# Memory queries and half of the gates through the opening's quarter products; first convolution tap on ScalarE, product with the sigmoid on GpSimd

## The chip, the core and the metric

The kernel runs on one core of a Trainium2 chip, on five engines that each work through their own queue of instructions in order and wait for each other through semaphores: PE (TensorE, matmuls), DVE (VectorE), ACT (ScalarE), POOL (GpSimd) and SP (SyncE, which here issues the DMAs). The metric is the device time of one launch in microseconds.

## The reference

One layer of a decoder, in float32, over 1024 tokens of width 1024. What the change touches is the combined input projection and what is taken from it:

```python
u = rms_norm(h, norm_mix_pre[layer])
proj = u @ w_in[layer]
sb_qkv, z, xbc_raw, dt_raw, mem_q, gate_logits = jnp.split(proj, SPLIT_POINTS, axis=-1)
...
y_sb = stick_breaking_attention(to_heads(q), to_heads(k), to_heads(v))
# ssd_branch:
xbc = jax.nn.silu(causal_depthwise_conv(xbc_raw, conv_w, conv_b))   # 4 taps per channel
y = y.reshape(b, s, SSD_INNER) * jax.nn.silu(z)
y_mem = mem_cross_attention(mem_q, mem, norm_mem[layer], w_mem_kv[layer])
```

Stick-breaking attention weighs a key by `sigmoid(z)` times the product of `1 - sigmoid(z)` over the keys between it and the query; per head and per block of 128 queries that is a running product (a scan) along the keys. After the three branches come their merge, an output projection and an MLP.

## The kernel before, in words

`proj` has 96 blocks of 128 columns: q 0 to 7, k 8 to 15, v 16 to 23, z (the gates of the SSD branch) 24 to 39, x, B and C (the convolved ones) 40 to 63, the memory's queries 64 to 71, the merge's gate logits 72 to 95. Each float32 matmul is made as three passes on rounded halves (hi x hi, hi x lo, lo x hi), so a block of 128 columns over all 1024 tokens costs 8 x 3 x 2 = 48 matmuls of 128x512.

**The opening stage** (`front`, until about 336 us) normalizes x, transposes it, makes blocks 0 and 1, the decays and the memory's keys and values (16 items of 24 matmuls each), and then makes pairs of blocks with Strassen-like quarter products: the pair's 2x2 quarters come out of seven products p1 to p7 of 12 matmuls, 84 in place of 96. There are 11 pairs (blocks 2 to 23). POOL makes sums of weight quarters (`weight_sums`), ACT rounds them (`round_front`, `round_back`), DVE takes the rests (`rest_of_front`, `rest_of_back`) and adds the products up (`c11`, `make_u2`, ...).

**The stick-breaking stage** (`stick_breaking`, from about 336 to 1089 us) runs over 16 heads x 8 blocks of queries = 128 steps. Step i with t = i mod 8 (called t=0 to t=7 below) handles (t+1)*128 keys: PE makes the scores (L1301, `sb_psz`), ACT two sigmoids of them (L1395 into `sb_rest`, L1399 into `sb_beta`), DVE the scan over `sb_rest` (L1509), POOL the product of both (L1451). Two steps later PE transposes the weights (`turn`, L1260, `sb_pst`), ACT rounds them (L1362), DVE takes the rest (L1459, `sb_wtl`), each in units of up to four blocks over two PSUM buffers: a transpose waits until the rest of the unit two before is taken. Every four steps PE multiplies the weights with the values (`weigh_values`, L1317, `sb_psy`), and ACT and DVE (L1493) move that out.

Between these, PE makes the blocks 24 to 71 as direct products (`project`, L1279, `sb_psg`): 48 blocks, 48 matmuls each. The list AT_STEP says how many of them each step of a head gets: 11 at t=0 up to 25 at t=7, 144 a head. They stand in PE's program in two halves, one ahead of the step's transposes and one behind. Each kind of block has a tail that is put at steps counted from the one in which the block ends (`ends`): a convolved block ("x") is copied by ACT, then on DVE the first tap (L1469) and the second (L1473) one step later, the other two taps two steps later, a sigmoid on ACT three later (L1386), the product with it on DVE four later (L1479), the store five later. A gate block ("z") has its sigmoid on ACT and its product on DVE (L1484) at once; a query block ("q") is copied and stored. The order in every engine's program is fixed by these loops; within a step DVE has the scan, then the rests of the transposed weights, then the tails.

With 144 matmuls a head, three blocks end in each head: in t=3, t=5 and t=7. Kinds run "xzxzxq", so a convolved block ends at t=5 in one head and at t=3 and t=7 in the next. The weights' blocks come through a two-slot ring: SP loads, POOL rounds (L1429) and takes the rest (L1437).

The later stages (SSD, merge, output projection, MLP) read `scratch_proj` and are not touched.

## Time and profile before

| | us |
|---|---|
| median of 3 runs | 2694.46 (2691.84 to 2698.86) |
| the profiled execution | 2688.13 |
| its span | 2686.4 |
| opening stage up to the first step's block products | 0 to 336.5 |
| stick-breaking stage | 336.5 to 1088.9 |

The clock granted to PE over the profiled execution was 0.99 of full speed. In the page a group's row is: line, engine, operation, output<-inputs, shapes, count | busy us, mean ns of one | idle time of the engine before it and what ended it. A timeline row is: start us, length us, engine, line, operation, names, count, and in brackets the idle time before and what ended it. A row of the windows is: from:to in us, length; then for PE, PEld (weight loads), DVE, ACT and POOL the busy us and the number of instructions; then the clock granted to PE (1.00 is 2.4 GHz, 0.50 is 1.2 GHz), the share of time that DMA was busy, and GB/s. A matmul's length includes its way through the array; the time that it takes of PE is the distance from its start to the next one's.

### The profile page before, as it was taken

How to read it: one execution, taken by the hardware profiler on the slowest of the kernel's cores; microseconds unless marked ns; L12 is line 12 of the kernel's file. 1: busy time of each engine (PE TensorE's matmuls, PEld its weight loads, DVE VectorE, ACT ScalarE, POOL GpSimd, SP SyncE). 2: the span in 40 equal slices, each digit the busy share in tenths (PEclk: the TensorE clock that was granted, in tenths of full speed). 3: DMA queues.
4: the chain of work that ended last, by engine and by line, in shares of the span. 5: the costliest groups of instructions: out<-in, count | busy, mean ns of one | idle time of the engine just before them, and what ended most of it. 6: DMA issues, size and time to landing. Idle time of an engine off the chain costs nothing. (4 is left out here: it accounts for less than half of the span.)

```text
span 2686.4 us, 35512 instructions
## 1 busy us (share of the span) xinstructions
PE 2597.0 (97%) x12752; PEld 2175.4 (81%) x12752; DVE 1850.0 (69%) x2063; ACT 1191.2 (44%) x2098; POOL 1313.1 (49%) x809
## 2 busy tenths in 40 slices
PE   7999999999999999799999899999998999999998
PEld 6888888888888888688888777878887788888886
DVE  5666476777677677498888656653258887768567
ACT  5533144444444444467666544443144222244443
POOL 3233255454554554288888743545600676535224
PEclk9999999999999999899999999999999999999999
DMA  4634443433324341467666653434331444376574
GB/s 160 204 151 160 153 149 105 126 102 109 112 94 134 110 119 62 137 175 210 196 207 202 226 189 133 152 134 149 126 126 55 150 160 166 129 245 211 203 253 146
DMA packets 208108, 411.53 MB, mean 153 GB/s; under 512 B 19648, under 2 KB 100160, under 8 KB 207936
## 3 DMA queue, kind: packets, MB, share of 16 engines
q1 hardware_dynamic: 207936, 409.27, 46.0%
q8 instruction: 104, 1.70, 0.3%
q14 instruction: 68, 0.56, 0.1%
HBM read 289.01 MB, written 120.19 MB: 152 GB/s over the span
## 5 line engine op out<-in xcount | busy, mean ns | idle before, releaser
L1451 POOL TENSOR_TENSOR sb_beta<-sb_beta,sb_rest 128x128 f32<-128x128 f32 (+7 forms) x128 | 164.1, 1282 | 371.4 <-DVE sb_rest L1509 371.4
L1279 PE MATMUL sb_psg<-uh,sb_wl 128*128 128x512 f32 x768 | 309.7, 403 | 0.0
L1279 PE MATMUL sb_psg<-ul,sb_wh 128*128 128x512 f32 x768 | 304.3, 396 | 0.0
L1279 PE MATMUL sb_psg<-uh,sb_wh 128*128 128x512 f32 x768 | 302.8, 394 | 0.0
L3169 PE MATMUL ff_ps<-ff_mh,ff_total 128*128 128x512 f32 x896 | 278.6, 391 | 4.6 <-DVE ff_total L3672 4.6
L1509 DVE TENSOR_TENSOR_SCAN sb_rest<-sb_rest 128x128 f32<-128x128 f32 (+7 forms) x128 | 187.3, 1463 | 115.1 <-ACT sb_rest L1395 114.8
L3169 PEld LDWEIGHTS ff_ps<-ff_mh,ff_total 128*128 128x128 f32 x896 | 169.4, 189 | 41.0 <-issue 5.7
L2314 PE MATMUL first_ps<-uh,mg_wh 128*128 128x512 f32 x480 | 193.3, 403 | 6.2 <-DVE ul L2519 4.9
L2314 PE MATMUL first_ps<-ul,mg_wh 128*128 128x512 f32 x480 | 188.5, 393 | 0.0
L2314 PE MATMUL first_ps<-uh,mg_wl 128*128 128x512 f32 x480 | 188.3, 392 | 0.0
L3169 PE MATMUL ff_ps<-ff_ml,ff_total 128*128 128x512 f32 x448 | 175.2, 391 | 0.0
L1362 ACT ACTIVATE sb_wth<-sb_pst 128x512 fp32r<-128x512 f32 (+1 forms) x192 | 87.3, 490 | 189.9 <-PE sb_pst L1260 186.6
L1279 PEld LDWEIGHTS sb_psg<-ul,sb_wh 128*128 128x128 f32 x768 | 144.4, 188 | 29.9
L1279 PEld LDWEIGHTS sb_psg<-uh,sb_wl 128*128 128x128 f32 x768 | 144.6, 188 | 25.4
L1279 PEld LDWEIGHTS sb_psg<-uh,sb_wh 128*128 128x128 f32 x768 | 144.9, 189 | 24.0
L1801 PE MATMUL first_ps<-uh,ssd_gwh 128*128 128x512 f32 x384 | 155.0, 404 | 5.9 <-ACT ssd_out L1866 5.0
L1801 PE MATMUL first_ps<-ul,ssd_gwh 128*128 128x512 f32 x384 | 151.5, 395 | 0.0
L1801 PE MATMUL first_ps<-uh,ssd_gwl 128*128 128x512 f32 x384 | 151.2, 394 | 0.0
L1459 DVE TENSOR_TENSOR sb_wtl<-sb_pst,sb_wth 128x512 fp32r<-128x512 f32 (+1 forms) x192 | 99.6, 546 | 74.3 <-ACT sb_wth L1362 74.3
L2292 POOL TENSOR_TENSOR merged<-merged,mg_gate 128x1024 f32<-128x1024 f32 x24 | 61.3, 2553 | 159.6 <-DVE mg_gate L2526 159.6
L1473 DVE SCALAR_TENSOR_TENSOR sb_out<-sb_padded,sb_cw,sb_out 128x1024 f32<-128x1024 f32 x72 | 131.7, 1829 | 1.7
L1395 ACT ACTIVATE sb_rest<-sb_psz 128x128 f32<-128x128 f32 (+7 forms) x128 | 83.6, 653 | 108.6 <-PE sb_psz L1301 107.7
(422 smaller groups left out, 7259.6 us busy)
## 6 DMA issues: line engine op xcount, KB each, us to landing
sb_w<-in_w_in SPq DMA_DIRECT2D x48, 512.0 KB, 4.4
scratch_proj<-sb_out SPq DMA_DIRECT2D x48, 512.0 KB, 2.9
ff_w<-in_w_down SPq DMA_DIRECT2D x96, 256.0 KB, 3.4
sb_k<-scratch_qk SPq DMA_DIRECT2D x64, 256.0 KB, 6.1
ssd_arow<-scratch_decay SPq DMA_DIRECT2D x32, 512.0 KB, 5.6
mg_gate<-scratch_proj SPq DMA_DIRECT2D x32, 512.0 KB, 3.6
ff_w<-in_w_up SPq DMA_DIRECT2D x32, 512.0 KB, 3.7
mg_w<-in_w_branch SPq DMA_DIRECT2D x30, 512.0 KB, 4.5
```

Of the source, the lines that this page charges most:

```text
L1279: last = nc.tensor.matmul(ps_g[:, h], l[:, s, k], r[:, k, h * HALF:(h + 1) * HALF], start=(k == 0 and j == 0), stop=(k == KB - 1 and j == 2))
L1362: nc.scalar.activation(out, src, ACT.Copy).then_inc(hi_done, 1)
L1395: nc.scalar.activation(rest[:, i % 3, 1:cols + 1], ps_z[:, 0:cols], ACT.Sigmoid, scale=-0.125).then_inc(keep_done, 1)
L1451: nc.gpsimd.tensor_tensor(beta[:, i % 3, 0:cols], beta[:, i % 3, 0:cols], rest[:, i % 3, 0:cols], ALU.mult).then_inc(weighted, 1)
L1459: nc.vector.tensor_tensor(out, src, hi, ALU.subtract).then_inc(lo_done, 1)
L1473: nc.vector.scalar_tensor_tensor(out_tile[:, 0], padded[:, tap:tap + S], cw[:, n, tap:tap + 1], out_tile[:, 0], ALU.mult, ALU.add).then_in ...
L1509: nc.vector.tensor_tensor_scan(kept, kept, kept, 1.0, ALU.mult, ALU.bypass).then_inc(scanned, 1)
L1801: last = nc.tensor.matmul(ps_g[:, h], l[:, s, k], r[:, k, h * HALF:(h + 1) * HALF], start=(k == 0 and j == 0), stop=(k == KB - 1 and j == 2))
L2292: nc.gpsimd.tensor_tensor(merged[:, n % KB], merged[:, n % KB], gate[:, n % 2], ALU.add).then_inc(summed, 1)
L2314: last = nc.tensor.matmul(ps[:, s, cols], l[:, k], r[:, k, cols], start=(k == 0 and j == 0), stop=(k == KB - 1 and j == 2))
L3169: done = nc.tensor.matmul(down_bank(p, local), l[:, columns(local)], r, start=(begins and c == 0 and j == 0), stop=(c == PAIRS - 1 and j = ...
```

## The change: what it does, and the diff

1. Eight pairs move from the stick stage to the opening: blocks 24 to 31 (half of the z gates) and 64 to 71 (the memory's queries). The opening has 19 pairs in place of 11. For the four gate pairs ACT takes the sigmoid and DVE multiplies, before the tile is stored.
2. The stick stage keeps 32 blocks, kinds "xxxz", 96 matmuls a head (AT_STEP 5 to 19). Two blocks end in each head: the first in t=5, the second in t=7. The first is always a convolved block; the second is one in every other head and a gate block in the rest.
3. The first tap goes from DVE to ACT (`first_tap`, an activation with scale and bias) in the step in which the block ends; DVE keeps one tap in the next step and two in the one after. The product with the sigmoid goes from DVE to POOL (`silu`), ahead of POOL's other work of its step. `padded` is doubled, and `out_tile` is used by the number of the block.
4. In the opening DVE's and ACT's order changes: the rest of a normalized tile is taken right behind its scaling, the decays are taken out one tile earlier in the loop, the third memory item's rest comes ahead of the first blocks' low halves, the rounding of the four sums of u (`round_t`) is spread over items 2, 5, 8, 11, and the first pair's factors are made at items 13 and 14.

```diff
+Z_EARLY = 8
...
-    BLOCK_PAIRS = [(b, b + 1) for b in range(2, Z0, 2)]
+    BLOCK_PAIRS = [(b, b + 1) for b in (*range(2, Z0 + Z_EARLY, 2), *range(MQ0, G0, 2))]
...
+    FIRST_GATED, N_GATED = (Z0 - 2) // 2, Z_EARLY // 2
...
+    T_ITEMS = (2, 5, 8, 11)
...
+        def sigm_of_tile(c, row):
+            act.wait_ge(c22_made if row else c11_made, c + 1)
+            act.wait_ge(c21_made if row else c12_made, c + 1)
+            act.wait_ge(hi_stored[row], 16 * N_SPLIT)
+            if c > FIRST_GATED:
+                act.wait_ge(gated, gates_to(c - 1, row))
+            nc.scalar.activation(sigm[:, row], tiles[:, 2 * (c % 2) + row], ACT.Sigmoid).then_inc(tile_sigm, 1)
...
+        round_kv(2)
         hi_of_first(0)
-        round_kv(2)
         hi_of_first(1)
         for m in range(N_KV):
-            if 1 <= m <= 4:
-                round_t(m)
+            if m in T_ITEMS:
...
-            if m == 15:
+            if m == 13:
                 round_front(0)
+            if m == 14:
+                for which in (S1, S2, S3):
+                    round_back(which, 0)
                 act.wait_ge(sumsT_out, 1)
                 nc.scalar.activation(grownT, sumsT, ACT.Exp).then_inc(grown_out, 1)
-        for which in (S1, S2, S3, A22, S4):
+        for which in (A22, S4):
             round_back(which, 0)
...
+            if c and is_gate(c - 1):
+                for row in range(2):
+                    sigm_of_tile(c - 1, row)
...
+        def gate_of_tile(c, row):
+            dve.wait_ge(tile_sigm, gates_to(c, row))
+            x = tiles[:, 2 * (c % 2) + row]
+            nc.vector.tensor_tensor(x, x, sigm[:, row], ALU.mult).then_inc(gated, 1)
...
-        for i in range(TILES + 2):
-            if i >= 3:
-                rest_of_u(i - 2)
-            if i < TILES:
-                invert(i)
-            if 0 < i <= TILES:
-                scale_turned(i - 1)
-            if i == 2:
+        for i in range(2):
+            invert(i)
+        scale_turned(0)
+        for i in range(1, TILES):
+            if i == 1:
                 rest_of_u(0)
-            if i == TB - 2:
+                scale_turned(1)
+                rest_of_u(1)
+                invert(2)
+            else:
+                scale_turned(i)
+                if i + 1 < TILES:
+                    invert(i + 1)
+                rest_of_u(i)
+            if i == TB - 3:
                 take_decays(0)
         rest_of_kv(0)
         rest_of_kv(1)
+        rest_of_kv(2)
         lo_of_first(0)
-        rest_of_kv(2)
         lo_of_first(1)
         take_decays(1)
         for m in range(N_KV):
-            if 1 <= m <= 4:
-                rest_of_t(m)
             if m + 3 < N_KV:
                 rest_of_kv(m + 3)
+            if m in T_ITEMS:
+                rest_of_t(T_ITEMS.index(m) + 1)
...
-            if m == 15:
+            if m == 13:
                 rest_of_front(0)
+            if m == 14:
+                for which in (S1, S2, S3):
+                    rest_of_back(which, 0)
                 dve.wait_ge(sums_turned, 1)
                 dve.wait_ge(first_stored, 64)
                 nc.vector.tensor_copy(sumsT, ps_csT).then_inc(sumsT_out, 1)
-        for which in (S1, S2, S3, A22, S4):
+        for which in (A22, S4):
             rest_of_back(which, 0)
...
-    rest, padded = sb("rest", [P, 3, S + 1]), sb("padded", [P, CONV - 1 + S])
+    rest, padded = sb("rest", [P, 3, S + 1]), sb("padded", [P, 2, CONV - 1 + S])
...
-    kinds = "xzxzxq"
+    kinds = "xxxz"
...
-    AT_STEP = (11, 13, 15, 17, 19, 21, 23, 25)
+    AT_STEP = (5, 7, 9, 11, 13, 15, 17, 19)
...
-        return {"x": p * 3 + X0 + x // 2, "z": p * 2 + Z0 + x // 2, "q": p + MQ0}[kinds[x]]
+        return X0 + convs_before(m) if kind_of(m) == "x" else Z0 + Z_EARLY + gates_before(m)
...
-                if i == ends(m, 1) + {"x": 5, "z": 2, "q": 1}[kind_of(m)]:
+                if i == ends(m, 1) + {"x": 5, "z": 2}[kind_of(m)]:
...
+        def first_tap(m):
+            n, s = convs_before(m), m % 2
+            act.wait_ge(drained[0], n + 1)
+            act.wait_ge(drained[1], n + 1)
+            if n == 0:
+                act.wait_ge(small_loaded, 32)
+            if m >= 2:
+                act.wait_ge(g_stored[s], (m // 2) * 16)
+            nc.scalar.activation(out_tile[:, s], padded[:, n % 2, 0:S], ACT.Identity, scale=cw[:, n, 0:1],
+                                 bias=cb[:, n:n + 1]).then_inc(tapped, 1)
...
-            act.wait_ge(conv_step, (m // 2 + 1) * CONV)
-            if m >= 2:
-                act.wait_ge(silu_done, m // 2)
-            nc.scalar.activation(sigm[:], out_tile[:, 0], ACT.Sigmoid).then_inc(sigm_done, 1)
+            n = convs_before(m)
+            act.wait_ge(conv_step, (n + 1) * TAPS)
+            if n:
+                act.wait_ge(silu_done, n)
+            nc.scalar.activation(sigm[:], out_tile[:, m % 2], ACT.Sigmoid).then_inc(sigm_done, 1)
...
+                if kind_of(m) == "x" and ends(m, 1) == i:
+                    first_tap(m)
...
+        def silu(m):
+            pool.wait_ge(sigm_done, convs_before(m) + 1)
+            nc.gpsimd.tensor_tensor(out_tile[:, m % 2], out_tile[:, m % 2], sigm[:], ALU.mult).then_inc(silu_done, 1)
...
+            for m in range(FILL):
+                if kind_of(m) == "x" and i == min(ends(m, 1) + 4, N - 1):
+                    silu(m)
...
-                if tap == 0:
-                    for h in range(2):
-                        dve.wait_ge(drained[h], m + 1 - gates_before(m))
-                    if n:
-                        dve.wait_ge(g_stored[0], n * 16)
-                    nc.vector.tensor_scalar(out_tile[:, 0], padded[:, 0:S], cw[:, n, 0:1], cb[:, n:n + 1],
-                                            ALU.mult, ALU.add).then_inc(conv_step, 1)
+                if tap == 1:
+                    dve.wait_ge(tapped, n + 1)
                 else:
-                    dve.wait_ge(conv_step, n * CONV + tap)
-                    nc.vector.scalar_tensor_tensor(
-                        out_tile[:, 0], padded[:, tap:tap + S], cw[:, n, tap:tap + 1],
-                        out_tile[:, 0], ALU.mult, ALU.add).then_inc(conv_step, 1)
-
-        def silu(m):
-            dve.wait_ge(sigm_done, m // 2 + 1)
-            nc.vector.tensor_tensor(out_tile[:, 0], out_tile[:, 0], sigm[:], ALU.mult).then_inc(silu_done, 1)
...
-                    convolve(m, range(2))
+                    convolve(m, range(1, 2))
                 if kind_of(m) == "x" and i == end + 2:
                     convolve(m, range(2, CONV))
-                if kind_of(m) == "x" and i == end + 4:
-                    silu(m)
                 for h in range(2):
                     if kind_of(m) == "z" and i == ends(m, h):
```

How the orders read, in three places.

DVE, stick stage, from the scan of t=7 to the rest of the weights of t=7 (`sb_wtl<-sb_pst 128x4x128 x2`, which the product with the values waits for); before, a head whose convolved block ended at t=5 (the operation named SCALAR_TENSOR_TENSOR on `sb_rest` is the scan):

```order
L1509 SCALAR_TENSOR_TENSOR sb_rest<-sb_rest 128x1024
L1459 TENSOR_TENSOR sb_wtl<-sb_pst,sb_wth 128x4x128
L1459 TENSOR_TENSOR sb_wtl<-sb_pst,sb_wth 128x2x128
L1473 SCALAR_TENSOR_TENSOR sb_out<-sb_padded,sb_cw,sb_out 128x1024 x2
L1509 SCALAR_TENSOR_TENSOR sb_rest<-sb_rest 128x128
L1459 TENSOR_TENSOR sb_wtl<-sb_pst,sb_wth 128x4x128
L1459 TENSOR_TENSOR sb_wtl<-sb_pst,sb_wth 128x3x128
L1509 SCALAR_TENSOR_TENSOR sb_rest<-sb_rest 128x256
L1459 TENSOR_TENSOR sb_wtl<-sb_pst,sb_wth 128x4x128 x2
```

The same place in the changed kernel, a head with two convolved blocks:

```order
L1565 SCALAR_TENSOR_TENSOR sb_rest<-sb_rest 128x1024
L1524 TENSOR_TENSOR sb_wtl<-sb_pst,sb_wth 128x4x128
L1524 TENSOR_TENSOR sb_wtl<-sb_pst,sb_wth 128x2x128
L1533 SCALAR_TENSOR_TENSOR sb_out<-sb_padded,sb_cw,sb_out 128x1024 x2
L1565 SCALAR_TENSOR_TENSOR sb_rest<-sb_rest 128x128
L1524 TENSOR_TENSOR sb_wtl<-sb_pst,sb_wth 128x4x128
L1524 TENSOR_TENSOR sb_wtl<-sb_pst,sb_wth 128x3x128
L1533 SCALAR_TENSOR_TENSOR sb_out<-sb_padded,sb_cw,sb_out 128x1024
L1565 SCALAR_TENSOR_TENSOR sb_rest<-sb_rest 128x256
L1524 TENSOR_TENSOR sb_wtl<-sb_pst,sb_wth 128x4x128 x2
```

DVE's list there is the same plus one tap. In the heads whose second block is a gate, a gate's product (`sb_out<-sb_psg,sb_out 128x512`) stands in front of the scan of t=0 instead of that tap.

PE, from the transposes of the weights of t=7 (at t=1) to the product with the values (L1317) at t=2, before:

```order
L1260 MATMUL sb_pst<-ident,sb_beta 128x128 x8
L1279 MATMUL sb_psg<-uh,sb_wl 128x512
L1279 MATMUL sb_psg<-uh,sb_wh 128x512
L1279 MATMUL sb_psg<-ul,sb_wh 128x512
L1279 MATMUL sb_psg<-uh,sb_wl 128x512
L1279 MATMUL sb_psg<-uh,sb_wh 128x512
L1279 MATMUL sb_psg<-ul,sb_wh 128x512
L1279 MATMUL sb_psg<-uh,sb_wl 128x512
L1301 MATMUL sb_psz<-sb_k,sb_q 128x384
L1300 MATMUL sb_psz<-sb_hiddenr,sb_identr 128x128
L1301 MATMUL sb_psz<-sb_k,sb_q 128x384
L1317 MATMUL sb_psy<-sb_wth,sb_v 128x512
```

The same place in the changed kernel:

```order
L1306 MATMUL sb_pst<-ident,sb_beta 128x128 x8
L1325 MATMUL sb_psg<-uh,sb_wl 128x512
L1325 MATMUL sb_psg<-uh,sb_wh 128x512
L1325 MATMUL sb_psg<-ul,sb_wh 128x512
L1325 MATMUL sb_psg<-uh,sb_wl 128x512
L1347 MATMUL sb_psz<-sb_k,sb_q 128x384
L1346 MATMUL sb_psz<-sb_hiddenr,sb_identr 128x128
L1347 MATMUL sb_psz<-sb_k,sb_q 128x384
L1363 MATMUL sb_psy<-sb_wth,sb_v 128x512
```

Four block products stand between the two where seven stood. From the scores of t=7 to the product with the values at t=2 there are 31 (19 + 5 + 7) where there were 49 (25 + 11 + 13); up to the transposes of the weights of t=7 there are 27 where there were 42.

DVE in the opening, around the decays (COPY), before:

```order
L870 TENSOR_TENSOR fr_f_hi<-fr_ps,fr_gains 128x1024
L887 COPY fr_p<-fr_ps 32x512
L876 TENSOR_TENSOR ul<-fr_f_hi,uh 128x8x128
L854 RECIPROCAL fr_stats<-fr_stats 128x1
L858 TENSOR_SCALAR fr_f_sums<-fr_f_back,fr_stats 128x1024
```

and in the changed kernel:

```order
L882 RECIPROCAL fr_stats<-fr_stats 128x1
L886 TENSOR_SCALAR fr_f_sums<-fr_f_back,fr_stats 128x1024
L904 TENSOR_TENSOR ul<-fr_f_hi,uh 128x8x128
L915 COPY fr_p<-fr_ps 32x512
L898 TENSOR_TENSOR fr_f_hi<-fr_ps,fr_gains 128x1024
```

The rest of the tile (`ul`), for which PE's next products wait, no longer stands behind the copy of the decays, which itself waits for 24 matmuls of PE.

## Rows read from the trace of the kernel before

**Rows 1.** Page, part 1: busy us (share of span) and instructions.
```profile
PE 2597.0 (97%) x12752; PEld 2175.4 (81%) x12752; DVE 1850.0 (69%) x2063; ACT 1191.2 (44%) x2098; POOL 1313.1 (49%) x809
```
**Rows 2.** Windows: opening's slow spell, its steady pairs, the whole stick stage.
```profile
46.60:48.00 1.40, 1.40 (x7) 1.40 (x8) 1.36 (x3) 0.00 (x0) 0.00 (x0) 0.54 0.00 0
48.00:50.00 2.00, 2.00 (x11) 2.00 (x11) 0.88 (x2) 1.44 (x2) 1.40 (x2) 0.50 0.00 0
150.00:200.00 50.00, 50.00 (x222) 41.44 (x221) 33.23 (x41) 17.23 (x24) 12.44 (x9) 1.00 0.50 190
336.50:1088.90 752.40, 750.12 (x3812) 631.22 (x3811) 537.82 (x518) 337.55 (x610) 377.87 (x222) 1.00 0.35 109
```
**Rows 3.** Waits of PE, 336 to 1090: waited for, us, times, longest.
```profile
PE sb_psz L1301 <- ACT sb_beta L1399: 1.9, 1, 1.9
PE sb_psy L1317 <- DVE sb_wtl L1459: 0.4, 1, 0.4
```
**Rows 4.** Timeline of PE, one passage: start, length, instruction [idle before].
```profile
609.46 0.39 PE L1301 MATMUL sb_psz<-sb_k,sb_q 128*128 128x512 f32 x1
...
610.49 0.39 PE L1279 MATMUL sb_psg<-uh,sb_wl 128*128 128x512 f32 x1
...
613.22 0.82 PE L1260 MATMUL sb_pst<-ident,sb_beta 128*128 128x128 f32 x6
...
622.24 1.04 PE L1260 MATMUL sb_pst<-ident,sb_beta 128*128 128x128 f32 x8
...
625.18 0.40 PE L1317 MATMUL sb_psy<-sb_wth,sb_v 128*128 128x512 f32 x1
```
**Rows 5.** Timeline of DVE, the same passage.
```profile
612.33 2.29 DVE L1509 TENSOR_TENSOR_SCAN sb_rest<-sb_rest 128x1024 f32<-128x1024 f32 x1
614.54 1.00 DVE L1459 TENSOR_TENSOR sb_wtl<-sb_pst,sb_wth 128x512 fp32r<-128x512 f32 x2
615.45 3.65 DVE L1473 SCALAR_TENSOR_TENSOR sb_out<-sb_padded,sb_cw,sb_out 128x1024 f32<-128x1024 f32 x2
619.02 0.42 DVE L1509 TENSOR_TENSOR_SCAN sb_rest<-sb_rest 128x128 f32<-128x128 f32 x1
619.64 1.16 DVE L1459 TENSOR_TENSOR sb_wtl<-sb_pst,sb_wth 128x512 fp32r<-128x512 f32 x2 [0.20 <-ACT sb_wth L1362]
621.49 0.89 DVE L1509 TENSOR_TENSOR_SCAN sb_rest<-sb_rest 128x256 f32<-128x256 f32 x1 [0.69 <-ACT sb_rest L1395]
623.51 1.29 DVE L1459 TENSOR_TENSOR sb_wtl<-sb_pst,sb_wth 128x512 fp32r<-128x512 f32 x2 [1.14 <-ACT sb_wth L1362]
```
**Rows 6.** Timelines of ACT and POOL, the same passage.
```profile
610.69 1.03 ACT L1395 ACTIVATE sb_rest<-sb_psz 128x1024 f32<-128x1024 f32 x1 [2.53 <-PE sb_psz L1301]
...
619.87 1.06 ACT L1386 ACTIVATE sb_sigm<-sb_out 128x1024 f32<-128x1024 f32 x1
...
614.70 2.00 POOL L1451 TENSOR_TENSOR sb_beta<-sb_beta,sb_rest 128x1024 f32<-128x1024 f32 x1 [5.00 <-DVE sb_rest L1509]
```
**Rows 7.** Timelines of DVE and POOL, the same place one head later.
```profile
669.45 1.28 DVE L1473 SCALAR_TENSOR_TENSOR sb_out<-sb_padded,sb_cw,sb_out 128x1024 f32<-128x1024 f32 x1
...
672.43 4.49 DVE L1473 SCALAR_TENSOR_TENSOR sb_out<-sb_padded,sb_cw,sb_out 128x1024 f32<-128x1024 f32 x2
...
672.11 2.41 POOL L1437 TENSOR_TENSOR sb_wl<-sb_w,sb_wh 128x1024 fp32r<-128x1024 f32 x1
```
**Rows 8.** Groups by line, DVE in the stick stage.
```profile
L1469 DVE TENSOR_SCALAR sb_out<-sb_padded,sb_cw,sb_cb 128x1024 f32<-128x1024 f32 x24 | 41.0, 1706 | 3.2 <-DMA scratch_proj<-sb_out 3.2
L1479 DVE TENSOR_TENSOR sb_out<-sb_out,sb_sigm 128x1024 f32<-128x1024 f32 x24 | 46.3, 1927 | 0.0
L1484 DVE TENSOR_TENSOR sb_out<-sb_psg,sb_out 128x512 f32<-128x512 f32 x32 | 21.8, 680 | 0.0
```
**Rows 9.** Timeline of PE in the opening: two gaps.
```profile
46.59 0.48 PE L562 MATMUL fr_ps<-uh,fr_fh 128*128 128x256 f32 x1 [1.90 <-DVE ul L876]
...
126.24 0.47 PE L583 MATMUL fr_ps<-uh,fr_fh 128*128 128x512 f32 x1 [2.77 <-DVE fr_fl L905]
```

53 lines of the change are left out of this document (33 added, 20 removed).

## The prediction

> **What bounds the kernel now.** I read the page's busy shares first: PE is busy for 97% of the span, the next engine, DVE, for 69% [rows 1]. So the question is what PE does, and whether others begin to hold it up. Then windows by stage: the steady part of the opening has PE busy 50.00 of 50 us with 222 matmuls, and in the stick stage PE is busy 750.12 of 752.4 us [rows 2]. The waits say the same: PE waits 1.9 and 0.4 us there in all [rows 3]. Both stages are bound by PE's matmuls, so taking matmuls away shortens them, until another chain comes due first. Which one that is the averages hide (DVE is busy 537.82 of 752.4 us in the stick stage, 71% [rows 2]), so I read the timelines of one passage where DVE's work is densest: from the scores of t=7 at 609.46 to PE's product with the values at 625.18 [rows 4 to 6].
>
> In it PE comes to the product at 625.18 - 609.46 = 15.72 us. What it needs then, the rest of the weights of t=7 on DVE, ends at 623.51 + 1.29 = 624.80, that is at 15.34 [rows 5]. The slack is 0.38 us. Of the 15.34 us DVE idles only 0.20 + 0.69 + 1.14 = 2.03 us, waiting for ACT, which waits for PE; and its scan of t=7 starts at 612.33 though ACT had delivered at 610.69 + 1.03 = 611.72 [rows 5, 6]. So DVE's own chain could be done at 15.34 - 2.03 = 13.31, and 0.61 us earlier still if it were free for the scan at once: 12.70.
>
> **The change part by part.** *Matmuls taken from the stick stage.* 16 blocks x 48 = 768. Twelve of them stand between 610.49 and 613.22 [rows 4]: 0.2275 us each, 174.7 us.
>
> *Matmuls added to the opening.* 8 pairs x 84 = 672, at 50 / 222 = 0.2252 us [rows 2]: 151.3 us. Net -23.4 us. This holds if the pairs stay bound by PE: in the steady window DVE is busy 33.2 and ACT 17.2 of 50 us, 2.6 pairs long. A gate pair asks two sigmoids (1.06 each [rows 6]) and two products (1.93 on DVE [rows 8]), in the places where the q and k pairs have two roundings and two subtractions; a query pair asks none of it. Cost zero; if that cover failed, 4 x 3.9 = 15 us. The two weight loads per pair go on at the same pace behind SP.
>
> *Opening's order.* The PE gap of 1.90 us before 46.59 is DVE's copy of the decays standing ahead of the rest of the tile; it goes. Behind it PE ran at a granted clock of 0.50 (1.2 GHz), from 46.6 to 50 us [rows 2, 9], which costs half of 3.4, about 1.7 us; it goes too. The gap of 2.77 us before 126.24 [rows 9] goes because the first pair's factor is made at item 13. Against it, the third tile is now scaled for transposing only behind a rest on DVE, ahead of PE's first products: its eight transposes (1.04 us when warm [rows 4]), about +1.4 at the start's slower pace. Together -5 (bounds -9 to +2; what is late next is the transposes' own chain). ACT's table for the sigmoid is loaded in the opening in place of the 1.9 us wait of rows 3: -1.
>
> *Tails in the stick stage.* DVE loses 24 first taps (41.0 us), 24 products (46.3) and 16 of 32 half gate products (10.9) [rows 8]; 537.8 - 98.2 = 440 us remain, for a stage of 752.4 - 174.7 = 578 us: 76%, where it was 71%. ACT gains 24 x 1.06 = 25 us and stays below 65%. POOL loses 16 blocks' rounding and rests, gains 24 products at about 2.0 (its product of the same shape took 2.00 [rows 6]) and stays near 63%. No engine becomes the bound on average.
>
> *The dense passage.* The blocks end at t=5 and t=7, so the two late taps still stand at t=7, DVE's list from there to the rest of the weights of t=7 is as before, and none of the 98 us was in it. PE's path through it loses 18 matmuls: 15.72 - 18 x 0.2275 = 11.62. DVE's chain: in heads whose second block is a gate, 12.70 + 0.68 (the gate's product [rows 8]) = 13.4, a wait of 1.8 us. In heads with two convolved blocks one tap of 1.28 [rows 7] joins it: 14.0, a wait of 2.4, and POOL's moved product now runs just there. What that costs DVE the trace shows for other POOL work: two taps alone are 2 x 1.28 = 2.56 us; the pair at 615.45 took 3.65, with POOL's product running for 1.25 us of it (until 616.70), and the pair at 672.43 took 4.49, with POOL busy for 2.09 us of it [rows 5 to 7]. So DVE stands still for about nine tenths of such an overlap. With 2.0 us of it the wait is up to 4.3; I take 3.0, as the product starts only when ACT's sigmoid is done and may fall on rests from PSUM. Sum: 8 x 1.8 + 8 x 3.0 = 38.4 us. Bounds: 0.7 and 1.3 a head if no POOL work falls on DVE's taps (16 us), 2.9 and 5.5 if all of it does (67 us).
>
> *Clock.* A gap of 1.90 us was followed by a clock of 0.50 [rows 2, 9]. The new waits are split over two places, the transposes and the product, so most single gaps are shorter; I count the slow spell in 4 of 16 heads, 4 x 1.7 = 6.8 us (bounds: none, and all 16, 27 us).
>
> The Trainium skill (SBUF — State Buffer, section Who interferes with whom) says that a DVE instruction with two SBUF inputs and a GpSimd instruction that reads SBUF exclude each other: the one issued second blocks until the first is through. The trace agrees (3.65 and 4.49 for 2.56). By the rule a product moved from DVE to POOL does not free DVE where a tap or scan falls under it, which speaks against this part of the change; it is the second rival below, worked out there from rows.
>
> **Sum.** -174.7 + 151.3 - 5 - 1 + 38.4 + 6.8 = +15.8 us. The profiled execution took 2688.13, so 2704 in its terms; the median of the three runs lies 6.3 us above it, so I forecast 2694.46 + 15.8 = 2710 as median.
>
> **The rivals.**
> *Faster: DVE keeps up.* If the taps at t=6 and t=7 meet no POOL work they take 1.28 each, and the waits are 0.7 and 1.3 us a head, 16 us in all, with no slow clock: -29.4 + 16 = -13.4, 2681. For it: DVE loses 98 us, and POOL has fewer blocks to round. Against it: POOL's product of t=7 must follow the scan of t=7 and so lies on the taps, as in rows 5 and 6. It decides from a mean wait of 29.4 / 16 = 1.84 us a head downwards.
> *Slower still: POOL shuts DVE out each time.* The rest of the next block on POOL (2.41 [rows 7]) falls on the tap at t=6 and puts off the scan of t=7 by 1.1, and the moved product lies fully on the tap at t=0: waits of 2.9 and 5.5 us, 67 us, with a slow clock in half the heads 13.6: -29.4 + 80.8 = +51, 2746. For it: the order of POOL's list puts the rest behind the product of t=6 and the moved product at t=1 and t=3. Against it: ACT's sigmoid waits for the taps and may let it start late.
> *PE's sum alone.* No new waits at all: -29.4, 2665. It would need DVE's chain done at 11.62, 1.1 us under its shortest.
> *The change does not do what it says* in the opening: gate pairs late on DVE, up to +15 on any of these; I give it no chance of its own.
>
> **How the numbers follow.** Forecast 0.55, with its own range 2696 to 2726; DVE keeps up 0.25; shut out 0.15; PE's sum alone 0.05. The range 2679 to 2742 leaves out the last and the far half of the third. About 0.3%, 8 us, is what a measurement of this kernel can tell from no change, so faster is below 2686: the first rival's lower part, the last and a little of the forecast's tail, 0.26. Same, 2686 to 2703: 0.21, the first rival's upper part and the forecast's lower. Slower 0.53.
>
> **What would show it.** Right: the stick stage about 578 + 45 = 623 us long; PE waiting in it for DVE's `sb_wtl` before the transposes and the product with the values, once a head, for some 40 us; a granted clock below 1.00 in a few slices; the opening's pair part 151 us longer with PE busy throughout; the gaps at 46.59 and 126.24 gone. Wrong: a stage near 580 with PE busy all along (then DVE's chain was mis-sized), waits at other steps than t=1 and t=2 (another chain), PE gaps among the gate pairs (the opening's cover), or waits for POOL's weights (`sb_wl`), which I price at nothing.

## The result, and the profile after

| | before | after |
|---|---|---|
| median, us | 2693.77 (4 runs, 2691.84 to 2698.86) | 2775.65 (4 runs, 2767.73 to 2776.38) |
| ratio | | 1.0294, 95% interval 1.0271 to 1.0318 |
| span of the profiled execution | 2686.4 | 2774.0 |

The changed kernel is 82 us slower. I had forecast 16 slower, with 2742 as the range's upper end, so the direction was right and the size lies outside the range. The page's first part for the changed kernel (busy us, share of the span, instructions), against [rows 1]:

```profile
PE 2604.8 (94%) x12656; PEld 2169.8 (78%) x12656; DVE 1892.0 (68%) x2111; ACT 1247.7 (45%) x2154; POOL 1369.0 (49%) x833
```

PE has 96 matmuls fewer and is busy 7.8 us longer, so some of them took longer. By the first and last matmul of each stage (us; "forecast" is the sum's terms for that stretch):

| stretch | before | after | difference | forecast |
|---|---|---|---|---|
| up to the first pair | 126.2 | 127.3 | +1.1 | -5 |
| pairs | 210.3 | 361.8 | +151.5 | +151.3 |
| stick stage, first to last projected block | 752.0 | 670.9 | -81.1 | -130.5 |
| from there to SSD's first matmul | 22.4 | 30.9 | +8.5 | 0 |
| SSD | 426.1 | 432.2 | +6.1 | 0 |
| the rest | | | +1.5 | 0 |

The windows' row of the stick stage (start:end, length, then busy us of PE, PEld, DVE, ACT and POOL, granted clock, DMA share, GB/s), against [rows 2]:

```profile
489.00:1160.40 671.40, 603.06 (x3044) 497.92 (x3044) 482.78 (x454) 347.81 (x601) 384.09 (x212) 0.97 0.32 97
```

DVE's work there fell from 537.8 to 482.8 us, by 55 where the operations taken from it were 98: what it kept became 43 us slower. And PE's waits from 489 to 1172, against the 2.3 us of [rows 3]:

```profile
PE sb_psy L1363 <- DVE sb_wtl L1524: 30.8, 13, 3.0
PE sb_pst L1306 <- DVE sb_wtl L1524: 25.2, 15, 2.5
PE sb_psg L1325 <- POOL sb_wl L1495: 8.6, 8, 1.2
PE sb_pst L1306 <- POOL sb_beta L1516: 6.5, 1, 6.5
PE sb_psz L1347 <- ACT sb_beta L1455: 4.6, 2, 4.0
```

So PE does now wait where the prediction looked: before the product with the values (`sb_psy`) and before the transposes (`sb_pst`), for DVE's rests of the weights. How one such passage runs is in DVE's timeline of one head (start, length, instruction), against [rows 5]:

```profile
606.35 3.35 DVE L1533 SCALAR_TENSOR_TENSOR sb_out<-sb_padded,sb_cw,sb_out 128x1024 f32<-128x1024 f32 x1
...
610.22 2.27 DVE L1565 TENSOR_TENSOR_SCAN sb_rest<-sb_rest 128x1024 f32<-128x1024 f32 x1
612.41 0.98 DVE L1524 TENSOR_TENSOR sb_wtl<-sb_pst,sb_wth 128x512 fp32r<-128x512 f32 x2
613.33 3.64 DVE L1533 SCALAR_TENSOR_TENSOR sb_out<-sb_padded,sb_cw,sb_out 128x1024 f32<-128x1024 f32 x2
...
618.27 3.34 DVE L1533 SCALAR_TENSOR_TENSOR sb_out<-sb_padded,sb_cw,sb_out 128x1024 f32<-128x1024 f32 x1
621.53 0.68 DVE L1565 TENSOR_TENSOR_SCAN sb_rest<-sb_rest 128x256 f32<-128x256 f32 x1
622.13 1.25 DVE L1524 TENSOR_TENSOR sb_wtl<-sb_pst,sb_wth 128x512 fp32r<-128x512 f32 x2
```

in POOL's, the same head, against [rows 6, 7]:

```profile
606.20 2.41 POOL L1495 TENSOR_TENSOR sb_wl<-sb_w,sb_wh 128x1024 fp32r<-128x1024 f32 x1
612.57 2.00 POOL L1516 TENSOR_TENSOR sb_beta<-sb_beta,sb_rest 128x1024 f32<-128x1024 f32 x1 [3.96 <-DVE sb_rest L1565]
...
618.13 2.39 POOL L1500 TENSOR_TENSOR sb_out<-sb_out,sb_sigm 128x1024 f32<-128x1024 f32 x1 [0.30 <-ACT sb_sigm L1442]
```

and in PE's, against [rows 4]:

```profile
618.03 1.06 PE L1306 MATMUL sb_pst<-ident,sb_beta 128*128 128x128 f32 x8 [1.21 <-DVE sb_wtl L1524]
...
623.44 0.51 PE L1363 MATMUL sb_psy<-sb_wth,sb_v 128*128 128x512 f32 x1 [2.95 <-DVE sb_wtl L1524]
```

A tap alone takes 1.28 us [rows 7]. Here the one at t=6 (606.35) takes 3.35, as POOL's rest of the next block runs from 606.20 to 608.61, and the one at t=0 (618.27) takes 3.34, as POOL's moved product runs from 618.13 to 620.52. Behind it stand the scan and the rests that PE waits for at 623.44. POOL takes its full time for both (2.41 and 2.39 us) while DVE's tap stands still.

The tap at t=0 takes 3.34 us in all eight heads with two convolved blocks. The tap at t=6 is caught in five of them (3.26 to 3.36 us); in the other three it starts first and takes 1.27 or 1.28, and POOL's rest takes 3.41 to 3.42 in place of 2.41. In the heads whose second block is a gate there is no tap at t=0, and the moved product falls on the scan of t=1, which alone takes 0.68 us for this shape:

```profile
577.73 2.36 POOL L1500 TENSOR_TENSOR sb_out<-sb_out,sb_sigm 128x1024 f32<-128x1024 f32 x1
578.24 2.39 DVE L1565 TENSOR_TENSOR_SCAN sb_rest<-sb_rest 128x256 f32<-128x256 f32 x1
```

It does so behind all seven of these heads that another head follows (2.39 to 2.46 us).

Two further costs show in rows. The first is the clock. After a gap of 2.48 us before the transposes at 578.01, PE runs at a granted clock of 0.50 (1.2 GHz), and is back at full speed 3 us later:

```profile
575.00:578.00 3.00, 0.53 (x3) 0.11 (x2) 2.96 (x6) 1.60 (x3) 0.64 (x2) 0.94 0.16 42
578.00:581.00 3.00, 2.99 (x11) 2.74 (x12) 3.00 (x3) 1.19 (x2) 2.38 (x2) 0.50 0.43 171
581.00:584.00 3.00, 3.00 (x14) 2.35 (x13) 1.77 (x3) 0.87 (x2) 0.86 (x2) 1.00 0.93 333
```

And at the end of the stage POOL waits 9.56 us with the last block's product, which stands in its list ahead of the last weighting. PE waits 6.5 us for that weighting (`sb_beta` in the waits above); before, it waited 1.5 us at this place, for DVE's rests:

```profile
1163.30 2.34 POOL L1500 TENSOR_TENSOR sb_out<-sb_out,sb_sigm 128x1024 f32<-128x1024 f32 x1 [9.56 <-ACT sb_sigm L1442]
1165.60 2.00 POOL L1516 TENSOR_TENSOR sb_beta<-sb_beta,sb_rest 128x1024 f32<-128x1024 f32 x1
```

### The profile page after: what moved, and what is told of

It is laid out like the page before. It is cut to its first block and busy times, and to the rows that moved or that the text cites. A ratio compares the mean times of both kernels' runs of the same rounds, so it can differ in the third digit from the quotient of the medians.

```text
span 2774.0 us, 35593 instructions
## 1 busy us (share of the span) xinstructions
PE 2604.8 (94%) x12656; PEld 2169.8 (78%) x12656; DVE 1892.0 (68%) x2111; ACT 1247.7 (45%) x2154; POOL 1369.0 (49%) x833
## 5 line engine op out<-in xcount | busy, mean ns | idle before, releaser
L1516 POOL TENSOR_TENSOR sb_beta<-sb_beta,sb_rest 128x128 f32<-128x128 f32 (+7 forms) x128 | 184.5, 1444 | 262.8 <-DVE sb_rest L1565 262.8
L1565 DVE TENSOR_TENSOR_SCAN sb_rest<-sb_rest 128x128 f32<-128x128 f32 (+7 forms) x128 | 222.8, 1741 | 99.6 <-ACT sb_rest L1451 99.4
L1325 PE MATMUL sb_psg<-uh,sb_wh 128*128 128x512 f32 x512 | 205.2, 401 | 8.6 <-POOL sb_wl L1495 8.6
L1325 PE MATMUL sb_psg<-uh,sb_wl 128*128 128x512 f32 x512 | 212.2, 414 | 0.0
L1325 PE MATMUL sb_psg<-ul,sb_wh 128*128 128x512 f32 x512 | 205.5, 401 | 0.0
L597 PE MATMUL fr_ps<-fr_t,fr_back 128*128 128x512 f32 x684 | 158.1, 389 | 0.0
L597 PEld LDWEIGHTS fr_ps<-fr_t,fr_back 128*128 128x128 f32 x684 | 128.4, 188 | 26.7
L1533 DVE SCALAR_TENSOR_TENSOR sb_out<-sb_padded,sb_cw,sb_out 128x1024 f32<-128x1024 f32 x72 | 139.3, 1935 | 0.8
L3014 POOL TENSOR_TENSOR ff_f_vl<-ff_w,ff_f_vl 128x512 f32<-128x512 f32 x48 | 76.9, 1612 | 110.6 <-DMA ff_w<-in_w_down 110.5
```

Of the source, the lines that this page charges most:

```text
L597: done = nc.tensor.matmul(bank(p, c), l[:, k * P:(k + 1) * P], r[:, k], start=(k == 0 and j == 0), stop=(k == Q - 1 and j == 2))
L1325: last = nc.tensor.matmul(ps_g[:, h], l[:, s, k], r[:, k, h * HALF:(h + 1) * HALF], start=(k == 0 and j == 0), stop=(k == KB - 1 and j == 2))
L1516: nc.gpsimd.tensor_tensor(beta[:, i % 3, 0:cols], beta[:, i % 3, 0:cols], rest[:, i % 3, 0:cols], ALU.mult).then_inc(weighted, 1)
L1533: nc.vector.scalar_tensor_tensor(out_tile[:, s], padded[:, n % 2, tap:tap + S], cw[:, n, tap:tap + 1], out_tile[:, s], ALU.mult, ALU.add). ...
L1565: nc.vector.tensor_tensor_scan(kept, kept, kept, 1.0, ALU.mult, ALU.bypass).then_inc(scanned, 1)
```

## The experiments

All thirteen, in the order in which they ran. "Stage" is first to last projected block of the stick stage, "waits" PE's from its start to the last product with the values (e13: to its last projected block). Each ratio is to runs of the kernel before that were made beside it (medians 2693.6 to 2697.8), so it can differ slightly from the quotient of two rows here. Where a part of the work is cut to 8 columns (e1, e2, e3, e12) the kernel leaves out part of the computation; such a run tells times only. A diff shows the lines that matter, with `...` and comments where it is shortened.

| run | total, us | ratio (95%) | stage | waits |
|---|---|---|---|---|
| before | 2693.8 | | 752.0 | 5.3 |
| after | 2775.7 | 1.029 | 670.9 | 75.7 |
| e1 small rest | 2747.9 | one run | 648.8 | 60.8 |
| e2 small product | 2731.2 | one run | 629.1 | 46.0 |
| e3 no late taps | 2754.9 | one run | 649.8 | 57.9 |
| e4 both on DVE | 2768.4 | 1.0277 (1.0249 to 1.0305) | 674.2 | 67.2 |
| e5 before + both moved | 2700.5 | 1.0023 (1.0013 to 1.0033) | 753.4 | 9.4 |
| e6 fills at t=7 | 2780.3 | 1.0326 (1.0310 to 1.0341) | 678.6 | 76.8 |
| e7 product later | 2742.4 | 1.0183 (1.0168 to 1.0199) | 642.9 | 51.8 |
| e8 product on DVE | 2728.9 | 1.0135 (1.0118 to 1.0152) | 633.6 | 46.2 |
| e9 one tap a step | 2724.0 | 1.0100 (1.0082 to 1.0118) | 634.3 | 44.5 |
| e10 and other slots | 2722.1 | 1.0095 (1.0078 to 1.0111) | 625.5 | 38.9 |
| e11 old tile order | 2770.1 | one run | 671.6 | 76.4 |
| e12 bare chain | 2701.1 | one run | 596.4 | 16.6 |
| e13 queries only | 2743.2 | 1.0183 (1.0169 to 1.0197) | 720.9 | 40.2 |

**e1: POOL's rest of a block made small.**

```diff
+            e = D if m < 2 else 8
-            nc.gpsimd.tensor_tensor(ring.lo[:, s].rearrange(flat), ring.raw[:, s], ...
+            nc.gpsimd.tensor_tensor(ring.lo[:, s].rearrange(flat)[:, 0:e], ring.raw[:, s, 0:e], ...
```

> GpSimd's second pass over each streamed block (the subtraction that makes the low part) takes 8 columns of 1024 instead of all, so the low parts of the stick stage's projected blocks are left out; everything else is the changed kernel. In the changed kernel that pass (2.4 us) runs over the tap at t=6, which takes 3.35 us there. Theory 1 (GpSimd shuts VectorE out, and that pushes VectorE's chain at t=7 past the product with the values): the tap at t=6 falls to about 1.3 us, the product's wait of 2.95 us per head falls to about 1, the stage from 671 us to about 650. Rival (the chain scan, two taps, rests is too long by itself for a path that lost fills): the tap is shorter but the waits stay, stage 665 to 672.

DVE's timeline in that run, same head:

```profile
605.24 1.28 DVE L1534 SCALAR_TENSOR_TENSOR sb_out<-sb_padded,sb_cw,sb_out 128x1024 f32<-128x1024 f32 x1
...
616.16 1.27 DVE L1534 SCALAR_TENSOR_TENSOR sb_out<-sb_padded,sb_cw,sb_out 128x1024 f32<-128x1024 f32 x1
617.36 2.85 DVE L1566 TENSOR_TENSOR_SCAN sb_rest<-sb_rest 128x256 f32<-128x256 f32 x1
```

The tap at t=6 is 1.28 us, and the stage 22 us shorter, both as theory 1 has it. But the product's wait did not shrink (35.8 us in all, 30.8 before this edit). DVE comes to its tap at t=0 earlier, so in six of the eight heads with two convolved blocks the moved product no longer falls on it but on the scan behind it: 2.85 us for 0.68. In the other two it still falls on the tap (3.35 us). A lock taken off one instruction landed on the next. The 22 us are not the tap's alone: the 8.6 us of waits for POOL's late weights are gone too, since it is those rests that were made small.

**e2: the moved product made small.**

```diff
-nc.gpsimd.tensor_tensor(out_tile[:, m % 2], out_tile[:, m % 2], sigm[:], ALU.mult)
+nc.gpsimd.tensor_tensor(out_tile[:, m % 2, 0:8], out_tile[:, m % 2, 0:8], sigm[:, 0:8], ALU.mult)
```

> The product with the sigmoid on GpSimd takes 8 columns of 1024, so the projected convolution blocks are left unmultiplied for the rest. The moved product (2.4 us) runs over the tap at t=0 (3.35 us) and the scan of t=1. Theory 1: that tap falls to about 1.3 us, the wait of 1.2 us for the low halves at t=0 to 1 and the wait of 1.4 to 2.5 us in gate heads shrink, the product's 2.95 us at t=7 shrinks by up to 1, the stage goes from 671 us to 650 to 658. Rival (the chain's length alone): stage 667 to 672. The 6.5 us gap at the end of the stage, where the last product holds GpSimd for the sigmoid, stays in both.

```profile
614.30 1.27 DVE L1533 SCALAR_TENSOR_TENSOR sb_out<-sb_padded,sb_cw,sb_out 128x1024 f32<-128x1024 f32 x1
615.50 0.69 DVE L1565 TENSOR_TENSOR_SCAN sb_rest<-sb_rest 128x256 f32<-128x256 f32 x1
```

The tap at t=0 is 1.27 in place of 3.34 us, the wait before the product with the values 0.89 in place of 2.95: 2.07 and 2.06, the same. POOL's weights are no longer late either. The stage is 41.8 us shorter, more than the 13 to 21 I gave it, as most of the slow clock went too: PE's busy time in the stage is 588.6 us in place of 603.1. In this run the moved product makes about half of the loss (2731 us in place of 2776). 46 us of waits remain.

**e3: taps 2 and 3 made small.**

```diff
+                e = S if tap == 1 else 8
-                    out_tile[:, s], padded[:, n % 2, tap:tap + S], ...
+                    out_tile[:, s, 0:e], padded[:, n % 2, tap:tap + e], ...
```

> Taps 2 and 3 of the convolution take 8 columns of 1024, so two of its four terms are left out. It removes some 3.6 us that stand between the scan and the rests on VectorE at t=7 (and at t=1). Both theories: the product's wait of 2.95 us goes and the stage comes to 625 to 632 us (PE's busy 603 and what is left of slow clock). If the waits at t=7 come from something else (transfers, the sigmoids on ScalarE), the stage stays over 655.

A miss: 649.8, not 625 to 632, though 3.6 us a block left DVE. The product on POOL now fell on the scan of t=1, in heads of both kinds (2.86 and 2.58 us):

```profile
615.95 2.86 DVE L1566 TENSOR_TENSOR_SCAN sb_rest<-sb_rest 128x256 f32<-128x256 f32 x1
...
615.05 3.20 POOL L1500 TENSOR_TENSOR sb_out<-sb_out,sb_sigm 128x1024 f32<-128x1024 f32 x1 [1.05 <-ACT sb_sigm L1442]
```

The waits before the transposes went (25.2 to 1.2 us), those before the product with the values stayed (36.7).

**e4: both operations back on DVE.** The edit is the diff's own, taken back: `convolve` makes tap 0, and `silu` is DVE's at `end + 4`.

> The changed kernel with the first tap and the product with the sigmoid both back on VectorE: what is left of the change is the moved blocks and the opening's order. Theory 1 (GpSimd's moved product costs by shutting VectorE out, some 2 us per conv block, against 1.28 us and 1.2 us that VectorE gets back to do): the two cancel, 2765 to 2785 us. Rival A (the two moved operations cost more than they save): 2725 to 2755. Rival B (VectorE's length is all that counts): 2795 to 2830, since each conv block gives VectorE 2.3 us more.

The time is 2768 us, as theory 1 said, but the tie is made of two larger amounts; e8 shows them. Its waits moved ahead of the transposes:

```profile
PE sb_pst L1306 <- DVE sb_wtl L1515: 52.2, 23, 4.0
PE sb_psy L1363 <- DVE sb_wtl L1515: 10.4, 10, 1.7
```

**e5: only the two operations moved, on the kernel before.**

```diff
+                if kind_of(m) == "x" and ends(m, 1) == i:
+                    first_tap(m)          # ACT
-                if kind_of(m) == "x" and i == end + 4:
-                    silu(m)               # DVE
+                if kind_of(m) == "x" and i == min(ends(m, 1) + 4, N - 1):
+                    silu(m)               # POOL
```

> The kernel before with only the two moved operations: first tap on ScalarE, product with the sigmoid on GpSimd; all blocks and the opening stay as they were. Theory 1 (GpSimd's product shuts VectorE out, but that costs only where PE's path has no slack; before has 144 projected matmul slots a head and some 3 us of slack at t=7): 2690 to 2715 us. Rival A (the two operations cost by themselves, whatever the schedule): over 2725, as 24 blocks times 1.7 us and more. Rival B (they relieve VectorE and help): under 2688.

```profile
337.40:1091.40 754.00, 752.13 (x3812) 632.58 (x3812) 492.39 (x472) 365.67 (x634) 442.30 (x244) 1.00 0.36 108
```

PE stays busy 752.13 of 754.00 us. DVE's taps take 2233 ns on the mean there, longer than the 1935 ns of the changed kernel, and nothing comes of it. The total is some 6 us longer all the same. The stretch from the last projected block to SSD's first matmul is 30.1 us in place of 22.4, with one wait of 6.1 us for the weighting behind POOL's last product, where the kernel before has 1.5. So inside the stage the lock costs nothing as long as PE has its cover.

**e6: the slots moved to t=7, 0 and 1.**

```diff
-    AT_STEP = (5, 7, 9, 11, 13, 15, 17, 19)
+    AT_STEP = (11, 13, 5, 5, 7, 12, 18, 25)
```

> The changed kernel with its 96 projection slots a head dealt out as 11, 13, 5, 5, 7, 12, 18, 25 over t=0 to 7 instead of 5, 7, 9, 11, 13, 15, 17, 19: t=7, 0 and 1 together have 49 as in the kernel before, not 31; the blocks still end at t=5 and t=7. Theory 1 (VectorE's chain against PE's shortened path at t=7 to 1): 18 slots more, 4.1 us, cover the waits of 3.9 us a head; stage 671 us to 630 to 645, total 2735 to 2750, unless the thin steps t=2 to 4 show waits in their turn. Rival (the waits are set by GpSimd's product wherever the slots stand): above 2765.

A miss: 678.6, not 630 to 645. The waits before the product fell from 30.8 to 13.0 us and those for DVE's rests before the transposes went, as expected, but the stage grew. PE now reached a new block before POOL had its rest, and its PSUM half before DVE had multiplied the gate. The total is in the rival's range (above 2765), but not by the rival's cause:

```profile
PE sb_psg L1325 <- POOL sb_wl L1495: 23.0, 8, 2.9
PE sb_psg L1325 <- DVE sb_out L1540: 21.5, 7, 3.3
```

**e7: the product on POOL two steps later.** The sigmoid of a head's second block goes two steps later too, and the last block's product stands behind the last weighting.

```diff
-                if kind_of(m) == "x" and i == min(ends(m, 1) + 4, N - 1):
+                if kind_of(m) == "x" and i == product_at(m):     # ends(m, 1) + 6
```

> The changed kernel with GpSimd's product two steps later (at t=3 and t=5 of the next head in place of t=1 and t=3, with the sigmoid of the second block at t=4), and the last block's product behind the last weighting. Same work on each engine. Theory 1 (what counts is where GpSimd's product falls on VectorE): the product's waits of 2.95 us fall to about 0.9 as without the product, the 6.5 us gap at the end of the stage to about 2, stage 671 to 635 to 650, total 2735 to 2752. Rival (GpSimd's added load as such, wherever it stands): 2765 or more.

Both ranges met: stage 642.9, total 2742. The product's 2.95 us fell to 0.9, with the same work on every engine. So the place counts. The gap at the stage's end shrank from 6.5 us to 4.1, not to 2; what ends it is now DVE's rests, and the stretch up to SSD is 29.5 us in place of 30.9. The product still meets DVE's work: the one at 634.97 starts during a scan of 128x768 (633.97) and takes 3.86 us, not 2.4. The scan takes 2.67 us where such a one in the kernel before took 1.76, but not by the product: POOL's weighting had started ahead of it, and in e8, without any product on POOL, every second scan of this shape takes 2.4 to 2.7 us too.

**e8: the product back on DVE, the first tap still on ACT.**

```diff
-            nc.gpsimd.tensor_tensor(out_tile[:, m % 2], out_tile[:, m % 2], sigm[:], ...
+            nc.vector.tensor_tensor(out_tile[:, m % 2], out_tile[:, m % 2], sigm[:], ...
```

> The changed kernel with the product with the sigmoid back on VectorE, first tap still on ScalarE. Theory 1: no lock at t=0 and 1 from GpSimd, but some 1.3 us more of VectorE's own per block at the same steps; between the run without the product (2731) and the one with both operations back (2768): 2745 to 2762. Rival (the first tap on ScalarE is what costs): no better than 2768. Rival (GpSimd's place is free): slower than the changed kernel, over 2780.

The time is 2729 us, better than the 2745 to 2762 I expected. Against e4 it differs by the first tap alone, against the changed kernel by the product alone: on these blocks the first tap on ACT gives 39 us back, and the product on POOL costs 47 (37 of them in the stage and 3.6 between it and SSD; 7 lie in SSD and behind it, where nothing was edited). The change had a good and a bad half.

**e9 and e10: e8's work in another order.** e9 puts one tap in each of three steps; e10 takes that and `AT_STEP = (8, 10, 10, 10, 10, 12, 17, 19)`.

```diff
-                if kind_of(m) == "x" and i == end + 2:
-                    convolve(m, range(2, CONV))
+                if kind_of(m) == "x" and i == end + 2:
+                    convolve(m, range(2, 3))
+                if kind_of(m) == "x" and i == end + 3:
+                    convolve(m, range(3, CONV))
```

> As the run with the product back on VectorE (2729 us, stage 633.6 us), but with taps 1, 2 and 3 in three successive steps instead of 1 and then 2 with 3; sigmoid and product one step later each. Same work on each engine. Theory 1 (what is left is VectorE's chain between the scan of t=7 and the scan of t=0, in which two taps of 1.8 us and a gate's product stand): the waits for the low halves at t=0 to 1 (31.9 us in all, 1.2 to 3.0 each) fall to 15 or less, stage 605 to 618, total 2700 to 2715. Rival (VectorE's sum counts, not its order): 2724 to 2735.

> The run before with the 96 slots a head dealt out as 8, 10, 10, 10, 10, 12, 17, 19: blocks end at t=4 and t=7, and t=0 and 1 have 6 slots more, taken from t=2 to 5. Theory 1: with the block's end away from t=5, its taps fall on t=5, 6 and 7 and not on 6, 7 and 0; the waits left at t=0 to 1 shrink by the 6 slots (1.4 us a head at most) if nothing thin shows in the middle: 2685 to 2708 us, and it could meet the kernel before. Rival (the middle steps starve in their turn, as seen when the slots were all put at t=7): 2715 or more.

In e9 the waits before the transposes fell from 31.9 to 13.5 us, and those before the product rose from 8.4 to 25.8: the rival (the sum counts, not the order) is right. The total is 2724, at the lower end of its range, and theory 1's 2700 to 2715 was missed. e10 has a stage 9 us shorter than e9's, from a block's end at t=4 and the slots moved to t=0 and 1 together; the total gained 2 us of it, as SSD and what follows, which were not edited, took 8 us longer. It is the fastest version of the changed kernel with all its work, still 1% over before, above the 2685 to 2708 of theory 1 and in the range of the rival. Its middle steps did not starve, though: its waits are DVE's rests, as in e9.

**e11: DVE's old order over the opening's tiles.** The edit puts the loop of before back (the diff's first hunk in `vector`).

> The changed kernel with VectorE's order over the first eight tiles of the opening as before (the rest of the opening's order stays changed). If VectorE's new order makes the third turn wait 8.2 us instead of 4.5, this brings it back to 4.5 and the first pair comes some 2 to 5 us earlier than 127.3 us, at 122 to 125; if it is ScalarE's order or the loads, it stays at 8.2 and 127 to 129.

PE's row behind the third wait in the changed kernel, and in this run:

```profile
22.61 1.76 PE L567 MATMUL fr_ps<-ident,fr_f_sums 128*128 128x128 f32 x7 [8.19 <-DVE fr_f_sums L886]
```

```profile
21.74 0.55 PE L576 MATMUL fr_ps<-uh,fr_fh 128*128 128x256 f32 x1 [4.59 <-DVE ul L904]
```

The wait is back at 4.59 us and the first pair at 125.3, just outside the 122 to 125 I expected. With the changed order the first pair stood at 126.3 to 129.7 in the other runs, so that order costs 1 to 4 us here.

**e12: all of DVE's taps and POOL's product made small.** The edits of e2 and e3 together, tap 1 too.

> The changed kernel with all three taps on VectorE and the product on GpSimd cut to 8 columns of 1024 (three of four terms of the convolution and its gating are left out). It asks what the waits are made of that stay at 39 to 46 us in sum in four runs, however VectorE's work was ordered (without the product 46.0, product on VectorE 46.2, one tap a step 44.5, with other slots 38.9). Theory 1 (VectorE's convolution work in the way of scans and low halves): with it gone the waits fall under 15 us and the stage to 577 to 592 us. Rival (the round trip scores, sigmoids, scan, weighting, turn, copies, product is itself longer than PE's path once 48 matmuls a head are gone): waits stay at 30 us or more, stage 608 us or more.

```profile
PE sb_psz L1347 <- ACT sb_beta L1455: 6.6, 2, 6.0
PE sb_psy L1363 <- DVE sb_wtl L1524: 6.0, 16, 1.4
PE sb_pst L1306 <- POOL sb_beta L1516: 4.0, 1, 4.0
```

The rival falls: the five engines' round trip alone costs 6 us in 16 heads. Theory 1's own ranges were missed by a little (waits 16.6 us for under 15, stage 596.4 for 577 to 592). So nearly all of the waits in e1 to e4 and e7 to e10 are the convolution's work, DVE's own or POOL's on top; e6 has its own two, shown there. And the total is 2701, in one run, no better than before (2689.9 to 2698.4 in the runs beside it): even with this work nearly gone the moved blocks do not beat the kernel before.

**e13: only the queries moved.** e8 with `Z_EARLY = 0`, kinds "xzxxz", 120 slots a head, the old tile order.

> Only the memory queries (8 of the 16 blocks) go to the opening's quarter products, all gates stay in the stick stage: 120 projected slots a head of eight steps (8, 10, ... 22) in place of 96; product on VectorE, first tap on ScalarE, VectorE's order over the first tiles as in the kernel before. By the rows PE alone gives 192 x 0.2275 back for 168 x 0.2252, 5.8 us less than before. Theory 1 (loss comes only once PE's path is shorter than the chain; before has 3 us of slack at t=7 and loses 1.9 of it here): 2685 to 2698 us. Rival (any step that loses slots loses time): 2705 or more.

A miss (2743, not 2685 to 2698), and my sum in it was wrong: 8 blocks are 384 matmuls, so PE alone gives 384 x 0.2275 - 336 x 0.2252 = 11.7 us, not 5.8. The stage was 720.9 us where 752.0 - 87.4 = 664.6 was to be had. But the run does not decide between its two theories, since it has a fault of its own, in ACT's waits of the stage:

```profile
ACT sb_out L1419 <- DMA scratch_proj<-sb_out: 48.5, 8, 7.2
```

With five blocks in two heads a gate's slot still holds a convolved block whose store is not done, and ACT stands 6 us in front of it, its taps and sigmoids behind. Whether a smaller move would have stayed inside the slack is open.

## Why the prediction was wrong

Step by step, by the terms of its sum.

- *Matmuls.* Right: +151.5 for +151.3 in the opening, where PE stayed busy throughout. Gate pairs cost nothing there.
- *The dense passage, 38.4 us: the step that failed.* Its chain and its two places were right, and so was the rate of the lock, nine tenths of the overlap. What failed is how much of POOL's work it let fall on DVE's. Measured are 56.0 us at the two places, on the mean 4.1 us in a head of two convolved blocks (forecast 3.0) and 2.9 in one with a gate (1.8). In the first kind I took a middle value between "no POOL work on a tap" and "all of it", on the hope that ACT's sigmoid would come late. It comes 0.3 us after POOL is ready, and in all eight heads the product lies on the tap in full (e2: 2.07 us a head), so there was no middle to take. In the second kind I had no POOL work at all, yet the product lies on the scan of t=1 behind each of them but the last; without it PE's wait before the product with the values is at most 0.18 us there (e2) where it is up to 1.47. POOL's rest of the next block, on the tap at t=6, was set aside as well. In heads where that tap is caught PE waits 1.2 to 1.5 us before the transposes, in the others 0.8; the 22 us of e1 hold more than that.
- *The rival "POOL shuts DVE out each time"*, to which I gave 0.15, came nearer: 67 us for the 56.0. Part of that is luck. It has 5.5 us in a head of two convolved blocks, where 4.1 was measured, and its 2.9 in the heads with a gate is met although its cause for them (a tap at t=6 kept waiting for all of POOL's rest) is not there: those taps take 1.27 to 1.76 us, and it did not have the scan of t=1 either. Its total of 2746 is 30 us short, as it too leaves out what follows here.
- *POOL's weights, priced at nothing*: 8.6 us, once in each head pair. The moved product stands in POOL's list ahead of the next block's rounding; e2 and e8, without it on POOL, have none of them.
- *The start of the stage*, 1 us off the 1.9: 4.6 instead, so 3.7 over. The table is indeed no longer loaded there, but ACT waits 7.27 us before 502.30 for a store of the opening's tiles (3.30 us before 349.60 in the kernel before), and PE waits 3.96 us for ACT behind it. No run was made on it.
- *Clock, 6.8 us*: about 18, and 10 more that are not the clock. PE's busy time in the stage is 603.1 where 750.1 - 174.7 = 575.4 was to be had: 27.7 us. The granted clock is 0.50 in nine places of the stage, 37.5 us in all, and PE is busy for 35.3 of them, so the clock costs half of that, 17.6 us. I had four such places, because the waits were split; yet single ones reach 2.5 and 2.95 us, and five of the eight of 2.95 us are followed by it. The other 10 us are the waits themselves, an estimate from rows: the last matmul before a wait counts as busy with its way through the array (0.39 us in place of 0.23), and the first behind one holds PE for 0.34 in place of 0.23, 37 times in the stage. The prediction has no term for it. e12 bears this out: only 3.5 busy us at 0.50, and still 584.9, 9.5 over. The clock's part falls with the waits: 588.6 in e2, of which 9.4 at 0.50.
- *The end of the stage*, not in the sum: +8.5. That POOL's last product comes ahead of a weighting that it need not precede could be read in the diff, `min(ends + 4, N - 1)`. It is not the only cause. With the product on POOL and PE's old cover the stretch is 30.1 us (e5), with the product on DVE and the cover gone 27.3 (e8), before 22.4 and in the changed kernel 30.9: either alone brings most of it. With the product behind the last weighting (e7) it is 29.5, as PE then waits 4.1 us for DVE's rests.
- *Opening's order, -5*: +1.1. The gaps at 46.59 and 126.24 went as said, but the waits around the third tile grew from 0.98 + 4.45 to 8.19, by 2.8 us where I had 1.4, and five gaps of about 1 us are new. e11 shows the first. Against them, the two spells at half clock that the kernel before has in the opening are gone.
- *SSD, +6.1*: not foreseen, and not settled. SSD is 2 to 8 us over the one profile of before in all fourteen others, those with hardly a wait in the stick stage too (e5: 2, e12: 8), so it doesn't come from those waits. In the trace PE's waits for ACT's `ssd_out` grew from 5.0 to 8.3 us, about half of it; why they did is open, and so is how far the one profile of before is typical.

The over-run of 72 us is thus 18 + 9 + 4 waits, 11 clock, 10 stopping and starting, 6 opening, 8.5 stage's end, 6 SSD, 1.5 later; 74 as rounded here, and the rest is the windows' ends. Theory 1 (POOL's product shuts DVE out, and that costs where PE's path has lost its cover) stands, but it is one of two costs, and the experiments size both in the stage: product on POOL 37 us (e8 against the changed kernel), convolution on DVE without enough cover 37 (e8 against e12). Against both stand the 23 us that PE's matmuls gain.

The Trainium skill (SBUF — State Buffer, section Who interferes with whom) has the exclusion of the two engines, and the traces agree with it: 3.35 and 3.34 us for a tap of 1.28 (changed kernel), 2.85 (e1) and 2.86 (e3) for a scan of 0.68. With POOL's work made small the same instructions take 1.28 and 0.69 (e1, e2). The second half of the prediction's doubt, that rests from PSUM might be hit instead, cost nothing in the trace: two of them at 612.41, with POOL's product over most of their time, took 0.98 us, between the 0.89 and 1.13 of the pairs of rests before and behind.

## What to carry to other kernels

Before taking work off the engine that bounds, measure what it covers: these blocks were 6% of PE's matmuls but hid DVE's convolution, and a net gain of 23 us was met by waits, slow clock and restarts of four times that. A product moved from VectorE to GpSimd frees VectorE only if nothing of VectorE that reads SBUF twice, taps or scans, runs at the same time; the tap moved to ScalarE was really gone from its path (39 us). When a cost depends on whether two fixed lists meet, take one case or the other, not the mean, and write the two lists side by side for each kind of head. Make a ceiling run (the suspected work cut to 8 columns) early: e12 alone would have told that no new order of this convolution could win by more than a few us, if at all.
